# A two-layer hybrid step on one core: history stores spread over the z steps, the sample convolution as products and one sum, squares moved one step earlier

## The reference, cut to what matters

```
u = za[..., :D_CONV] * sigmoid(za[..., D_CONV:])              # 1024 channels
u_ext = concat([prev_rows, u], axis=1)                        # 30 rows of history first
y = depthwise_conv(u_ext, conv_w) + conv_b                    # 31 taps per channel
y = silu(layer_norm(y, ln_g, ln_b))
state_conv = u_ext[:, -30:]                                   # an output, for prompt and samples
```

## Time and profile before

| | |
|---|---|
| median of 3 runs | 2968.92 us (2968.01 to 2970.41) |
| the profiled execution | 2969.42 us, span 2967.7 us |
| PE busy | 2789.3 us (94%) |
| DVE, ACT, POOL busy | 1400.8, 1162.6, 86.2 us |
| mean granted PE clock | 0.945 of full |

### The profile page before, as it was taken

One profiled execution on the slowest core, in us unless ns is written; L12 is line 12 of the kernel. 1 busy time (PEld: TensorE's weight loads), 2 busy tenths in 40 slices (PEclk: granted clock), 3 DMA queues, 4 the chain that ended last, 5 costly groups with the idle time before them and its releaser, 6 DMA issues.

```text
span 2967.7 us, 47943 instructions
## 1 busy us (share of the span) xinstructions
PE 2789.3 (94%) x20069; PEld 2550.5 (86%) x20069; DVE 1400.8 (47%) x2025; ACT 1162.6 (39%) x1488; POOL 86.2 (3%) x116
## 2 busy tenths in 40 slices
PE   5899968998999999999999899889899999999998
PEld 1688956787888878889899899569799999999998
DVE  1599735335444433344444535534544444445444
ACT  2333253234443322333443436433544433444433
POOL 1000000010000000000000100001000000000000
PEclk7999985799999999999999999579999999999999
DMA  9667782575777678877644444024344444444343
GB/s 387 276 261 281 276 141 84 195 279 213 280 284 284 254 304 321 300 278 279 252 149 158 154 170 165 16 70 156 137 163 155 153 156 164 170 170 170 132 167 129
DMA packets 75771, 603.50 MB, mean 203 GB/s; under 512 B 21029, under 2 KB 22373, under 8 KB 24050
## 3 DMA queue, kind: packets, MB, share of 16 engines
q1 hardware_dynamic: 75634, 601.54, 55.4%
HBM read 592.01 MB, written 9.49 MB: 203 GB/s over the span
## 4 chain that ended last, share of the span: by engine, by line
PE 86%; DMA 4%; DVE 4%; ACT 3%; issue 2%; SPq 1%; POOL 1%; DVEq 0%; POOLq 0%; ACTq 0%
PE ps L598 25%; PE ps L600 24%; PE ps L599 24%; PE ps L624 5%; DMA pre_ring<-in_w_ada 3%; DMA aring<-in_w_ada 2%; PE ps L797 1%; DVE w_lo L1316 1%; DVE cacc L1405 1%; PE ps L836 1%; SPq L455 1%; ACT tn L1130 1%; PE ps L637 0%; ACT w_hi L974 0%; PE ps L609 0%
## 5 line engine op out<-in xcount | busy, mean ns | idle before, releaser
L1316 DVE TENSOR_TENSOR w_lo<-raw,w_hi 128x2048 fp32r<-128x2048 f32 (+1 forms) x402 | 835.6, 2080 | 1159.5 <-ACT w_hi L974 1159.5
L598 PE MATMUL ps<-act_hi,w_hi 128*128 128x288 f32 x4352 | 1303.3, 299 | 45.3 <-DVE act_lo L1503 31.2
L599 PE MATMUL ps<-act_hi,w_lo 128*128 128x288 f32 x4352 | 1288.7, 296 | 0.0
L600 PE MATMUL ps<-act_lo,w_hi 128*128 128x288 f32 x4352 | 1284.1, 295 | 0.0
L974 ACT ACTIVATE w_hi<-raw 128x2048 fp32r<-128x2048 f32 (+1 forms) x402 | 699.4, 1741 | 1108.2 <-PE ps L600 1102.0
L598 PEld LDWEIGHTS ps<-act_hi,w_hi 128*128 128x128 f32 x4352 | 820.3, 188 | 106.4 <-issue 90.4
L600 PEld LDWEIGHTS ps<-act_lo,w_hi 128*128 128x128 f32 x4352 | 824.0, 189 | 0.0
L599 PEld LDWEIGHTS ps<-act_hi,w_lo 128*128 128x128 f32 x4352 | 822.1, 189 | 0.0
L598 PE MATMUL ps<-hid_hi,w_hi 128*128 128x288 f32 x1408 | 420.4, 299 | 8.6 <-DVE w_lo L1316 8.6
L599 PE MATMUL ps<-hid_hi,w_lo 128*128 128x288 f32 x1408 | 416.7, 296 | 0.0
L600 PE MATMUL ps<-hid_lo,w_hi 128*128 128x288 f32 x1408 | 415.3, 295 | 0.0
(11 more groups left out here) (263 smaller groups left out, 1442.5 us busy)
## 6 DMA issues: line engine op xcount, KB each, us to landing
aring<-in_w_ada SPq DMA_DIRECT2D x176, 1024.0 KB, 7.8
raw<-in_w_gu SPq DMA_DIRECT2D x88, 2048.0 KB, 8.2
raw<-in_w_dn SPq DMA_DIRECT2D x64, 1408.0 KB, 5.9
raw<-in_w_ab SPq DMA_DIRECT2D x20, 2048.0 KB, 8.0
raw<-in_w_out SPq DMA_DIRECT2D x16, 2048.0 KB, 8.2
raw<-in_w_cd SPq DMA_DIRECT2D x13, 2048.0 KB, 8.2
pre_ring<-in_w_ada SPq DMA_DIRECT2D x16, 1024.0 KB, 10.1
aring<-in_state_glaT SPq DMA_DIRECT2D x4, 1024.0 KB, 9.8
```

The source lines that it names most:

```text
L598: pe.matmul(bank, w_hi[:, h, cols], hi[:, kt, :], start=begin, stop=False)
L599: pe.matmul(bank, w_lo[:, h, cols], hi[:, kt, :], start=False, stop=False)
L600: mm = pe.matmul(bank, w_hi[:, h, cols], lo[:, kt, :], start=False, stop=end)
L1316: dve.tensor_tensor(w_lo[:, h, 0:w], raw[:, par, h * w:(h + 1) * w], w_hi[:, h, 0:w].bitcast(F32), ALU.subtract).then_inc(split_done, 1)
```

## The change

Four things are done.

1. **Stores.** A new `store_conv(ls)` on SP's list stands at the end of z steps 1, 2 and 3: the prompt's store and sample tiles 0 to 2, then 3 to 5, then 6 and 7. mix0 issues none.
2. **Sample convolution.** At tap 0 of a tile DVE makes four products of 8 x 31 overlapping rows with the 31 taps into a new `taps_prod` (128 x 992), ahead of the prompt's tap 0; just before tap 6 one `tensor_reduce` sums them to 32 columns; before tap 16 one `tensor_scalar` adds the bias. The 31 instructions of the samples go. The prompt's 31 stay.
3. **Squares.** In z step 1 `conv_squares` stands right behind ACT's high part of the next weights' first half (step 18, h = 0), and so ahead of the second half's; PE's `stat` stands behind the second half of z step 1 and no longer between the halves of step 2.
4. **Samples in one instruction.** The groups of 8 at L1540 (twice), L1154 and L1593 become one each, of 256 columns.

```
+            def store_conv(ls):
+                if ls == 1:
+                    sp.wait_ge(conv_ready, CT)
+                    sp.dma_start(o["conv_p"], uext[:, :, NP_TOK:UW]).then_inc(conv_stored, 16)
+                for j in range(3 * ls - 3, min(3 * ls, CT)):
+                    sp.dma_start(o["conv_s"][:, j], rows_s(j)[:, :, TS:SW]).then_inc(conv_stored, 16)
...
                     half(seg, n, par, 0, first and j == 0, hidden if j == 0 else None)
-                    if seg.kind == "z" and ls == 2:
-                        stat()
...
                     if seg.kind == "z" and ls == 0:
                         conv_mean()
+                    if seg.kind == "z" and ls == 1:
+                        stat()
...
+                    if seg.kind == "z" and ls == 1:
+                        act.wait_ge(centred, 1)
+                        conv_squares()
                     if seg.kind == "z" and ls == 2:
                         stat_rstd(CT * P)
...
                     epilogue(seg, n, par, ls)
-                    if seg.kind == "z" and ls == 1:
-                        act.wait_ge(centred, 1)
-                        conv_squares()
...
-                for s in range(NSEQ):
-                    ins = act.activation(act_hi[:, 0:CT, NP_TOK + TS * s:NP_TOK + TS * (s + 1)], y_all_s[:, :, s], ACT.Copy)
-                ins.then_inc(mixhi_done, CT)
+                act.activation(seqs8(act_hi[:, 0:CT, NP_TOK:T]), y_all_s, ACT.Copy).then_inc(mixhi_done, CT)
...
+                    ws = vec[:, bass.ds(j * TAPS + w, TAPS)].unsqueeze(1).to_broadcast([P, NSEQ, TAPS])
+                    for at_t in range(TS):
+                        ins = dve.tensor_tensor(taps_prod[:, at_t], rows_s(j)[:, :, at_t:at_t + TAPS], ws, ALU.mult)
+                    marks[1] = L.mark(ins)
                 for k in taps:
                     wk = flat_at(vec, j * TAPS + (w + k))
...
+                    if k == 6:
+                        L.wait(marks[1])
+                        marks[1] = L.mark(dve.tensor_reduce(acc_s, taps_prod[:], AX.X, ALU.add))
+                    if k == 16:
+                        L.wait(marks[1])
+                        dve.tensor_scalar(taps_s(j, 0).rearrange("p b t -> p t b"), acc_s, flat_at(vec, j + VEC["conv_b"]),
+                                          None, ALU.add)
...
+                    L.wait(marks[0])
+                    if k < TAPS - 1:
+                        marks[0] = L.mark(dve.scalar_tensor_tensor(acc, row, wk, acc, ALU.mult, ALU.add))
...
+                return dve.tensor_tensor(y_s, y_s, seqs(by[:, NP_TOK:T]).unsqueeze(1).to_broadcast([P, CT, NSEQ, TS]), op)
```

More of the change, by code:

```diff
@@ L80, in __init__ @@
         self.act_links = {"gate": 4, "gu": 4, "sgu": 8}.get(kind, 0)
-        self.dve_links = {"gate": 2 * TAPS - 1, "zconv": 2 * TAPS - 1, "gu": 2, "out": 4,
+        self.dve_links = {"gate": TAPS + 1, "zconv": TAPS + 1, "gu": 2, "out": 4,
                           "down": 2 if group else 4}.get(kind, 0)
@@ L269, in build @@
         with ExitStack() as a:
+            sb("under_z20", [P, 20 * T], stack=a)
+            taps_prod = sb("taps_prod", [P, TS, NSEQ, TAPS], stack=a)
+        with ExitStack() as a:
             tn = sb("tn", [P, 2, 4, T], stack=a)
@@ L349, in taps_s, with seqs8 @@
             return rows_s(j)[:, :, k:k + TS]
+        def seqs8(ap):
+            return ap.rearrange("p c (b t) -> p c b t", t=TS)
         y_all = uext[:, :, 0:NP_TOK]
@@ L438, in body @@
                         load_pair(pair_of(seg, ls))
+                    if seg.kind == "z" and ls:
+                        store_conv(ls)
+            def store_conv(ls):
[4 more added lines that the diff above has]
+                    sp.dma_start(o["conv_s"][:, j], rows_s(j)[:, :, TS:SW]).then_inc(conv_stored, 16)
             def open_layer0():
@@ L450, in mix0 @@
             def mix0():
[L452 to L455, removed]
                 for h in range(HEADS):
@@ L1388, in conv @@
                 w = VEC["conv_w"]
+                acc = cacc[:, 0:NP_TOK]
+                acc_s = cacc[:, NP_TOK:T].rearrange("p (t b) -> p t b", b=NSEQ)
                 if 0 in taps:
@@ L1393, in conv @@
                         L.wait(L.n)
+                    ws = vec[:, bass.ds(j * TAPS + w, TAPS)].unsqueeze(1).to_broadcast([P, NSEQ, TAPS])
+                    for at_t in range(TS):
+                        ins = dve.tensor_tensor(taps_prod[:, at_t], rows_s(j)[:, :, at_t:at_t + TAPS], ws, ALU.mult)
+                    marks[1] = L.mark(ins)
                 for k in taps:
                     wk = flat_at(vec, j * TAPS + (w + k))
[L1396 to L1409, removed]
+                    row = at(uext, j, k, k + NP_TOK)
+                    if k == 6:
[5 more added lines that the diff above has]
+                                          None, ALU.add)
+                    if k == 0:
+                        marks[0] = L.mark(dve.tensor_scalar(acc, row, wk, flat_at(vec, j + VEC["conv_b"]), ALU.mult, ALU.add))
+                        continue
+                    L.wait(marks[0])
+                    if k < TAPS - 1:
+                        marks[0] = L.mark(dve.scalar_tensor_tensor(acc, row, wk, acc, ALU.mult, ALU.add))
+                    else:
+                        dve.scalar_tensor_tensor(at(uext, j, 0, NP_TOK), row, wk, acc, ALU.mult, ALU.add).then_inc(conv_ready, 1)
             def ada_bias(u):
@@ L1590, in mix0 @@
                 dve.tensor_tensor(act_lo[:, 0:CT, 0:NP_TOK], y_all, act_hi[:, 0:CT, 0:NP_TOK].bitcast(F32), ALU.subtract)
[L1591 to L1594, removed]
+                dve.tensor_tensor(seqs8(act_lo[:, 0:CT, NP_TOK:T]), y_all_s, seqs8(act_hi[:, 0:CT, NP_TOK:T].bitcast(F32)),
+                                  ALU.subtract).then_inc(act_ready, CT)
                 dve.wait_ge(drained, Z_SEG.n0 + Z_SEG.steps)
```

## The result

The changed kernel takes 2955.74 us (median of 5 runs, 2952.32 to 2958.23), the kernel before beside it 2970.41 (5 runs): a ratio of 0.9949, 95% interval 0.9939 to 0.996, or some 15 us less. The forecast was 2955.8. The profiled execution of the changed kernel has a span of 2954.0 us.

A forecast was written before the change was run, and what follows sets the result against it. PE, busy 94% of the span, was taken as the bound, except in the opening (DVE) and around the z steps and mix0. Terms -16.0 + 2.4 + 2.1 - 1.6 = -13.1 us, from 2968.92 to 2955.8; range 2951 to 2961.

The forecast's parts named there:

- The wait, -16.0: Start of mix0: without DVE's and ACT's wait for the stores to land, it goes on at 430.62 instead of 446.62.
- The opening, +2.4: Opening convolution, where DVE is the chain: new products, sum and bias lengthen its first two tiles by 2.4 us.
- The draw in the gate steps: Gate steps: DVE's body rises from 28.90 to 29.70 us, level with PE's 29.70; PE stays the bound, 0.3 us left.
- The squares, +2.1: Before `stat`: PE idles 3.2 us, its clock falls, and ACT's high part comes at 393.1 instead of 391.05.
- Samples, -1.6: DVE's scaling, ACT's high part and DVE's low part of y, each in one instruction, save 0.48 + 0.63 + 0.48 us.
- The transfers: Steps 17 to mix0: at 3.6 us a store no load or pair is late, the pair of step 19 by 3 us.
- s: DMA time of one store, taken as 3.6 us, with bounds of 0.3 and 6.0.
- rival (d): From 5.8 us a store, state loads land 13 us behind need and all is lost; 2970 to 2971 at 6.0; chance 0.04.
- Rival (c): A store costs 4.5 us beside loads, so step 19's pair and the state come late; 2958 to 2962; chance 0.15.
- (a): PE's clock doesn't fall after the idle before `stat`, or the products are cheaper; 2952 to 2954; chance 0.15.
- (b): DVE becomes the bound of the gate steps, with products at twice the price; 2960.5; chance 0.12.
- (e): The stores' wait only gives way to another in mix0; none seen; counted under the others, chance 0.04 together.

The follow-up runs named there:

- stores_behind_states: The kernel before with its nine stores moved behind the first two state loads of the first mixer, nothing else; ratio to the kernel before 1.0007.
- products_twice: The changed kernel with the four products of each tile made twice, the second set into memory nothing reads; ratio to the kernel before 0.9981.
- after_again: The changed kernel run once more, unchanged; ratio to the kernel before 0.9957.
- squares_alone: The kernel before with only the squares and `stat` moved one step earlier; ratio to the kernel before 1.0006.
- stat_between_halves: The changed kernel with `stat` back between the halves of step 18, the squares left in their new place; ratio to the kernel before 0.9954.
- stores_one_each: The changed kernel with the old convolution, `stat` between the halves of step 18 and at most one store per z step; 2946.73 us, ratio to the kernel before 0.9924.

## Why the prediction was right, step by step

- **The wait, -16.0.** Shown: the stores alone gave 15.9, read against the one profile of the kernel before, and so good to some 2 us; their ratio allows 12 to 20. That it was the landing of the stores, and not the place of the state loads behind them, is shown by stores_behind_states.
- **The opening, +2.4.** It measured +2.2 in the changed kernel and alone. By section the low parts moved by 1.5 behind the first 16 taps (forecast 1.57), then by -0.1, by -0.55, by +1.8 (forecast 1.89) and by -0.4. The terms behind it held too: 0.51 to 0.52 us for a prompt tap alone, 1.40 and 1.39 for four products (1.36), 1.18 for the sum (1.17). The samples' 31 instructions had indeed cost almost nothing, since they lay in the latency of the prompt's chain.
- **The draw in the gate steps.** The bodies took 29.59 and 29.79 us against PE's 29.7, and PE waited for no low part there. That the reserve was small is shown by products_twice.
- **The squares, +2.1.** It measured +2.1 (4.3 less the opening's 2.2), and 2.05 alone; the idle 3.19, for 3.2. POOL's sum was ready 388.47 - 378.81 = 9.7 us after the first square, as forecast (384.3 - 374.6). By the rule of the Trainium skill in "SBUF — State Buffer", section "Who interferes with whom", POOL's copy waits for the DVE subtraction that began before it; the trace agrees, with 2.13 us for a copy that began at 379.39, 0.45 behind the low part at 378.94. The clock fell, but not where I had put it: just behind `stat`, so that `stat` took 0.75 and the loss lay in the half behind it. In after_again it fell ahead of `stat`, as forecast, but stayed low for 5.6 us and more and not for 3.3, and the term was +3.3 there (5.7 less the opening's 2.3). So the +2.1 came out in the first profile and in squares_alone, and one execution of the same kernel paid 1.2 us more; the term's size hangs on the single execution.
- **Samples, -1.6.** With the stores moved, 1.4.
- **The transfers: right in effect, wrong in one row.** From 359 to 414 us the engines moved nine stores, three pairs and two weights loads, so a store cost at most (55 - 5 x 5) / 9 = 3.3 us. That is a bound and no measurement of s: it shows that the forecast's 3.6 was high enough, and it rules out rival (d)'s 5.8. But the pair of step 19 was to be done at 405, 3 us ahead of need, and it came 3.4 us late. The step that failed is the start of that row of the chain: I let it begin when the engines were free, while SP could issue it only when PE had done with the pair before it, 397.11 + 1.92 = 399.0, and it then shared the engines with the load issued at 392.34 and two stores. It was in only some 16 us later, where the median of such a load is 8.2. It cost nothing in the changed kernel, since ACT and DVE were still at y and nobody waited for PE's second half; take away the idle before `stat`, and it costs 4 us (stat_between_halves, where ACT waits for it). Rival (c) had its symptom, a wait of PE for `in_w_ada` at 415, without its price.
- **Rivals.** (a) is excluded by the fall of the clock and by the products' 1.40 us; (b) by PE's waits, of which none from 170 to 260 us is for a low part; (d) by the state loads, which nobody waited for; (e) by `vtok`'s wait of 1.4 us for DVE's low part, the one foreseen.
- **The total.** -13.1 forecast; -13.0 by the trace at `vtok` (-11.7 in after_again), -14.7 by the medians, whose interval (0.9939 to 0.996, or -18 to -12) takes in both. That 2955.74 lies on 2955.8 to a tenth is luck: the kernel before itself had medians from 2967.6 to 2971.8 in the comparisons.

What stays open: the traces give 13.0 and 11.7 us and the medians 14.7; whether what lies between them is anything but scatter, these runs can't say.

## What to carry to other kernels

A store off the path isn't free: spread it so that each step gets one, right behind the loads that the step needs, and see to it that the issuing queue reaches no wait with a load behind it. Before small instructions are folded into fewer large ones, look whether they lie in the latency of a dependent chain; here 31 of them a tile cost about as little as nothing, and their replacement cost 0.7 us. And when a stall is removed by moving work earlier, ask whether the engine then stands before a new one with a shorter queue: the squares' move cost 2 to 3 us where the old place of `stat`, with the new place of the squares, gained 2 (stores_one_each), once the stores no longer made the pairs late.

## What the runs showed of the hardware

- A store of 1024 pieces of 120 bytes is dear in a row and cheap alone. Of three or eight in a row each takes SP 3.0 to 4.2 us to issue (12.59 / 3 = 4.2, 23.97 / 8 = 3.0) and the engines at most 3.3 (the changed kernel) to 3.6 us (the kernel before). One a step takes SP 0.4 to 0.6 us. A stretch of 30 us with two such stores has a DMA share of 0.81 to 0.83, one without has 0.73 to 0.75 in the kernel before from 230 to 350 us (one of its rows is below), which makes an estimate of 0.08 x 30 / 2 = 1.2 us each. The Trainium skill says in "DMA: Bandwidth & Descriptors", section "Why small descriptors are slow (HBM only)", that each small piece carries a fixed cost; the trace agrees in kind, as the same bytes at 403 GB/s would take 0.3 us.

```profile
290.00:320.00 30.00, 30.00 (x228) 26.80 (x228) 26.00 (x67) 8.85 (x8) 0.00 (x0) 1.00 0.73 280
```

- The same idle of PE, 3.2 us, was followed by the fall of the clock 0.8 us behind its end in one execution of a kernel and before its end in another. PE then worked at 0.50 for about 3.5 us in the first and for at least 5.6 us in the second, and the work up to the next high part took 1.2 us longer (8.75 us from the start of `stat`, and 9.96).
